# Decay and beta projection as the first, 16-pass unit of a token group, with tile products right behind the value projection

## The reference

```python
proj = rmsnorm(x) @ w_in          # q, k, v, gate z, beta logits (4), decay logits (4), attention q, k, v
qkv  = silu(causal_conv4(q, k, v))
beta = sigmoid(gb)                # 4 heads
g    = -exp(a_log) * softplus(ga + dt_bias)
o_gdn = chunked_delta_rule(q, k, v, g, beta)     # chunks of 64, cumulative sum of g in a chunk
o_gdn = rmsnorm(o_gdn) * silu(z)
o_att = sliding window attention (8 query heads, 2 key heads, window of 2 chunks, sinks)
x = x + concat(o_gdn, o_att) @ w_out
x = x + relu(rmsnorm(x) @ w1)**2 @ w2
```

## Time and profile before

| | us |
|---|---|
| median of 3 runs | 2410.79 (2410.4 to 2412.34) |
| the profiled execution, its own time | 2410.9 |
| its span | 2409.3 |
| TensorE busy in it | 2368.6 (98%) |
| VectorE busy | 1442.3 (60%) |
| ScalarE busy | 959.5 (40%) |

### The profile page before, as it was taken

The page is one execution under the profiler, slowest core; times in us unless marked ns, Lnnn a source line. Parts: engine busy times, 40 slices in busy tenths (PEclk is TensorE's granted clock), DMA queues, the critical chain, the costliest instruction groups (busy, mean ns, idle before and its releaser), DMA issues.

```text
span 2409.3 us, 36625 instructions
## 1 busy us (share of the span) xinstructions
PE 2368.6 (98%) x12654; PEld 1954.2 (81%) x12654; DVE 1442.3 (60%) x2125; ACT 959.5 (40%) x1719; POOL 154.2 (6%) x159
## 2 busy tenths in 40 slices
PE   6999999999999999999999999999999999999998
PEld 4888888888888888888888888888888888888886
DVE  6797662454679765255567966525456885642644
ACT  4476421223357532122346753212234664321222
POOL 0031000000003100000001200000000120000000
PEclk9999999999999999999999999999999999999999
DMA  4211222233321222223332122322432113222241
GB/s 152 96 62 63 96 96 96 96 130 123 106 79 63 80 96 97 96 96 135 118 106 70 63 88 88 104 96 94 141 119 95 68 54 105 88 98 97 92 152 66
DMA packets 63315, 232.63 MB, mean 97 GB/s; under 512 B 7392, under 2 KB 7520, under 8 KB 62544
## 3 DMA queue, kind: packets, MB, share of 16 engines
q1 hardware_dynamic: 55728, 201.98, 25.1%
q0 software_dynamic: 7456, 28.97, 3.5%
HBM read 222.54 MB, written 8.39 MB: 96 GB/s over the span
## 4 chain that ended last, share of the span: by engine, by line
PE 89%; DVE 7%; issue 2%; ACT 2%; DMA 0%; DVEq 0%; POOL 0%; ACTq 0%; POOLq 0%
PE ps L1421 87%; PE ps L1584 1%; PE ps L1647 1%; DVE nq L925 0%; DVE h_l L1357 0%; DVE acc L854 0%; DVE w_l L846 0%; DVE ti L1253 0%; DVE nq_l L930 0%; DVE state L1239 0%; DVE row L972 0%; DVE at L995 0%; DVE at L1011 0%; DVE qkvz L1022 0%; DVE qk L1014 0%
## 5 line engine op out<-in xcount | busy, mean ns | idle before, releaser
L1421 PE MATMUL ps<-h_h,w_h 128*128 128x512 f32 x2004 | 790.7, 395 | 11.3 <-DVE h_l L865 4.4
L1421 PE MATMUL ps<-h_l,w_h 128*128 128x512 f32 x2004 | 781.5, 390 | 0.0
L1421 PE MATMUL ps<-h_h,w_l 128*128 128x512 f32 x2004 | 781.5, 390 | 0.0
L846 DVE TENSOR_TENSOR w_l<-stage,w_h 128x1024 fp32r<-128x1024 f32 x381 | 466.4, 1224 | 256.9 <-ACT w_h L463 243.4
L463 ACT CAST w_h<-stage 128x1024 fp32r<-128x1024 f32 x381 | 398.3, 1045 | 544.2 <-PE ps L1421 543.8
L1421 PEld LDWEIGHTS ps<-h_h,w_h 128*128 128x128 f32 x2004 | 376.9, 188 | 106.7 <-DVE h_l L865 9.0
L1421 PEld LDWEIGHTS ps<-h_h,w_l 128*128 128x128 f32 x2004 | 377.0, 188 | 79.2
L1421 PEld LDWEIGHTS ps<-h_l,w_h 128*128 128x128 f32 x2004 | 377.3, 188 | 77.3 <-issue 1.9
L1421 PE MATMUL ps<-ff_h,w_h 128*128 128x512 f32 x1036 | 404.6, 391 | 0.0
L1421 PE MATMUL ps<-ff_h,w_l 128*128 128x512 f32 x1036 | 403.1, 389 | 0.0
L1421 PE MATMUL ps<-ff_l,w_h 128*128 128x512 f32 x1036 | 403.1, 389 | 0.0
(11 more groups left out here) (196 smaller groups left out, 1884.3 us busy)
## 6 DMA issues: line engine op xcount, KB each, us to landing
stage<-w SPq DMA_DIRECT2D x385, 512.0 KB, 3.3
x_next<-x POOLq DMA_DIRECT2D x20, 512.0 KB, 5.9
out<-xs POOLq DMA_DIRECT2D x32, 256.0 KB, 2.3
xs<-x POOLq DMA_DIRECT2D x8, 512.0 KB, 5.1
xs<-x POOLq DMA_DIRECT2D x4, 1024.0 KB, 5.4
bia<-bias POOLq DMA_DIRECT2D x1, 1024.0 KB, 5.0
cst<-con POOLq DMA_DIRECT2D x1, 448.0 KB, 3.9
cst<-con POOLq DMA_DIRECT2D x1, 192.0 KB, 3.3
```

Source lines behind the costliest of these rows:

```text
L846: dve.tensor_tensor(w_l[:, b, 0:k], stage[:, s, 0:k], w_h[:, b, 0:k].bitcast(F32), ALU.subtract).then_inc(w_lo.sem, 1)
L1421: return pe.matmul(o, a, b, start=start, stop=stop)
```

## The change

BA becomes unit 0 of a group and the convolution units are 1 to 12. BA's weight matrix holds the 8 used columns twice, at 0 to 7 and at 64 to 71; after the split a VectorE copy, `rows_low`, puts the low part of the second copy over columns 64 to 71 of the high buffer. BA then takes two passes per block instead of three (result rows 0 to 7 and 64 to 71, which the row chain adds). The whole row chain with its scans moves to the top of the group on VectorE and ScalarE, ahead of the convolution taps; the low part of convolution unit 1 stands inside it, that of unit 2 in the taps of unit 0. It works on 8 rows instead of 64 or 4. The four transposes of the rows and tile products 0 follow AV, then AK, tile products 1, AQ0, tile products 2, AQ1, tile products 3, AQ2, the 8 value transposes, AQ3. In VectorE's queue the last gate unit's low part moves behind `scatter`, and one pair of norm operations moves into `block_inverse`. ScalarE's load of the silu table moves behind its part of the row chain. The core of the diff (outer indentation taken off):

```diff
...
-U_BA, U_AV, U_AK, U_AQ, U_Z = 12, 13, 14, 15, 19
+U_BA, U_CONV, U_AV, U_AK, U_AQ, U_Z = 0, 1, 13, 14, 15, 19
 U_PAD, U_OUT, U_MLP = 23, 24, 32
...
-        R64, A4 = slice(0, 64), slice(32, 36)
-        X, E, U, L = (rw[R64, i] for i in range(4))
+        R = slice(0, 2 * HEADS)
+        X, E, U, L = (rw[R, i] for i in range(4))
...
+    split_hi(g, 0, 1)
+    act.wait_ge(unit_done.sem, unit_done.after(g, U_BA + 1))
+    act.activation(X, ps[R, A0, :], ACT.Identity, scale=prm[R, C_SGN:C_SGN + 1],
+                   bias=prm[R, C_DT:C_DT + 1]).then_inc(row_act.sem, 1)
+    act.wait_ge(row_dve.sem, row_dve.after(g, 2))
+    act.activation(E, E, ACT.Exp, scale=-1.0).then_inc(row_act.sem, 1)
+    split_hi(g, 0, 2)
+    act.wait_ge(row_dve.sem, row_dve.after(g, 4))
+    act.activation(L, U, ACT.Ln).then_inc(row_act.sem, 1)
+    act.wait_ge(row_act.sem, row_act.after(g, 3))
+    act.activation(U, L, ACT.Exp, scale=-1.0).then_inc(row_act.sem, 1)
...
     act.preload_act_table_set("silu_and_others")
...
+    def conv_input(i, s, split=True):
+        if split:
+            split_hi(g, i * 4, s + 2)
+        act.wait_ge(unit_done.sem, unit_done.after(g, i * 4 + s + 2))
+        act.copy(raw[:, s % 2, 3:], ps[:, A0 + (s + 1) % 2, :]).then_inc(raw_ready.sem, 1)
...
-        conv_input(0, s)
+        conv_input(0, s, s > 0)
...
-    split_hi(g, CONV, U_AV - CONV)
+    split_hi(g, CONV, U_AK - CONV)
...
+    act.wait_ge(vt_ready.sem, vt_ready.after(g, 1))
+    act.copy(avr[:, HD:], ps[:, A0 + 1, :]).then_inc(copied.sem, 1)
     tile(0)
+    split_hi(g, CONV, U_AQ - CONV)
     pack(0)
+    act.wait_ge(unit_done.sem, unit_done.after(g, U_AK + 1))
+    act.copy(akr[:], ps[:, A0, :]).then_inc(copied.sem, 1)
+    norm_hi(0)
+    tile(1)
+    split_hi(g, CONV, U_AQ + 1 - CONV)
...
-        if j < PAIRS - 1:
-            tile(j + 1)
+        if j < 2:
+            tile(j + 2)
         split_hi(g, CONV, U_AQ + 2 + j - CONV)
         norm_root(j)
-        if j < PAIRS - 1:
-            pack(j + 1)
+        if j < 2:
+            pack(j + 2)
+        if j == 2:
+            act.wait_ge(vt_sum.sem, vt_sum.after(g, 1))
+            act.copy(vt[:].rearrange("p c t k -> p c (t k)"), ps[:, PT:PT + 2, :]).then_inc(vt_ready.sem, 1)
     split_hi(g, CONV, U_Z + 2 - CONV)
     norm_root(PAIRS)
...
             pass_pad()
-        if m == GATE - 1:
...
+def rows_low(g, n):
+    own(w_lo, g, n + 1)
+    cols = slice(HD, HD + 2 * HEADS)
+    dve.tensor_copy(w_h[:, 0, :, cols], w_l[:, 0, :, cols].bitcast(F32)).then_inc(ba_lo.sem, 1)
...
 split_lo(0, 0)
+rows_low(0, 0)
 dve.wait_ge(N1["rt_ready"].sem, N1["rt_ready"].after(0, 1))
...
+    rd = [0]
+    def row_step(ins):
+        ins.then_inc(row_dve.sem, 1)
+        rd[0] += 1
+        own(row_dve, g, rd[0])
+    dve.wait_ge(unit_done.sem, unit_done.after(g, U_BA + 1))
+    dve.wait_ge(row_act.sem, row_act.after(g, 1))
+    row_step(dve.scalar_tensor_tensor(out=X, in0=ps[HD:HD + 2 * HEADS, A0, :],
+                                      scalar=prm[R, C_SGN:C_SGN + 1], in1=X, op0=ALU.mult, op1=ALU.add))
+    row_step(dve.scalar_tensor_tensor(out=E, in0=X, scalar=-1.0, in1=X, op0=ALU.mult, op1=ALU.max))
+    dve.wait_ge(row_act.sem, row_act.after(g, 2))
+    row_step(dve.tensor_scalar(U, E, 1.0, None, ALU.add))
+    row_step(dve.scalar_tensor_tensor(out=E, in0=U, scalar=-1.0, in1=E, op0=ALU.add, op1=ALU.subtract))
+    split_lo(g, 0, 2)
+    dve.wait_ge(row_act.sem, row_act.after(g, 4))
+    row_step(dve.tensor_tensor(E, E, U, ALU.mult))
+    row_step(dve.tensor_tensor(L, L, E, ALU.subtract))
+    row_step(dve.scalar_tensor_tensor(out=L, in0=X, scalar=0.0, in1=L, op0=ALU.max, op1=ALU.add))
+    row_step(dve.tensor_scalar(L, L, nalog[R], None, ALU.mult))
+    for t in range(TILES):
+        tile = slice(t * P, t * P + P)
+        row_step(dve.tensor_tensor_scan(row[R, tile], cst[R, K_ONE, :], rw[R, 3, tile], 0.0,
+                                        ALU.mult, ALU.add))
+    row_step(dve.tensor_copy(rowr[64:64 + 2 * HEADS], row[R]))
+    row_step(dve.tensor_tensor(rowr[96:96 + 2 * HEADS], row[R], rowr[64:64 + 2 * HEADS].bitcast(F32),
+                               ALU.subtract))
+    assert rd[0] == row_dve.per_group
+    dve.nop(nofuse=True)
     with dve.Fori(0, CONV // 4) as i:
...
-                    split_lo(g, i * 4, s + 2)
...
+    for t in range(TILES):
+        j = t - 2
         decay(t)
         diagonal(t)
         bias_column(t)
-        norm_square(j + 1)
-        norm_low(j + 1)
+        if t:
+            norm_square(j + 1)
+            norm_low(j + 1)
         products(t)
         split_lo(g, CONV, U_AQ + 2 + j - CONV)
         token_rows(t)
-        norm_apply(j)
+        if j >= 0:
+            norm_apply(j)
...
             if b == 8:
-                split_lo(g, CONV, U_Z + 2 - CONV)
-                norm_apply(PAIRS)
+                query(PAIRS - 1)
+                norm_apply(PAIRS - 1)
...
     gather()
-    query(PAIRS - 1)
-    norm_apply(PAIRS - 1)
+    query(2)
+    norm_apply(2)
     block_inverse()
+    split_lo(g, CONV, U_Z + 2 - CONV)
+    norm_apply(PAIRS)
+    scatter()
     split_lo(g, CONV, U_Z + 3 - CONV)
-    scatter()
...
+        if s == 15:
+            rows_low(g + 1, 0)
...
+    pe.wait_ge(w_lo.sem, w_lo.after(g, 1))
+    pe.wait_ge(ba_lo.sem, ba_lo.after(g, 1))
+    pe.nop(nofuse=True)
+    for k in range(KT):
+        n1_ready(k)
+        mm(ps[:, A0, :], w_h[:, 0, k], h_h[:, k], k == 0, False)
+        last = mm(ps[:, A0, :], w_h[:, 0, k], h_l[:, k], False, k == KT - 1)
+    last.then_inc(unit_done.sem, 1)
...
             pe.wait_ge(raw_ready.sem, raw_ready.after(g, (i * 4 + s) * 3 - 3))
-            unit(g, i * 4, s, A0 + s % 2, hid, first=n1_ready if s == 0 else None)
+            if s == 1:
+                pe.wait_ge(row_dve.sem, row_dve.after(g, 1))
+            unit(g, i * 4, s + 1, A0 + (s + 1) % 2, hid)
...
     pe.wait_ge(raw_ready.sem, raw_ready.after(g, 3 * CONV - 3))
-    unit(g, CONV, U_BA - CONV, A0, hid)
-    pe.wait_ge(raw_ready.sem, raw_ready.after(g, 3 * CONV))
     unit(g, CONV, U_AV - CONV, A0 + 1, hid)
-    pe.wait_ge(row_act.sem, row_act.after(g, 2))
-    unit(g, CONV, U_AK - CONV, A0, hid)
...
+        decay_rows(t)
         if t:
-            decay_rows(t)
...
+    pe.wait_ge(row_dve.sem, row_dve.after(g, row_dve.per_group))
+    pe.nop(nofuse=True)
+    for t in range(TILES):
+        last = pe.transpose(ps[:, ROWT, 64 * t:64 * t + 64], row[0:64, t * P:t * P + P], cst[0:64, K_ID, 0:64])
+    last.then_inc(B1["p_rowt"].sem, 1)
     tile_products(0)
+    pe.wait_ge(raw_ready.sem, raw_ready.after(g, 3 * CONV))
+    unit(g, CONV, U_AK - CONV, A0, hid)
+    tile_products(1)
     for j in range(PAIRS):
-        if j:
-            pe.wait_ge(copied.sem, copied.after(g, j + 1))
-        if j == 1:
-            pe.wait_ge(B1["tok"].sem, B1["tok"].after(g, 1))
+        pe.wait_ge(copied.sem, copied.after(g, j + 1))
         unit(g, CONV, U_AQ + j - CONV, A0 + (U_AQ + j) % 2, hid)
         norm_sum(j)
-        if j < PAIRS - 1:
-            tile_products(j + 1)
+        if j < 2:
+            tile_products(j + 2)
+        if j == 2:
+            wt(B["vb_r"], TILES - 1)
+            wt(B["kd_r"], TILES - 1)
+            for c in range(2):
+                for t in range(TILES):
+                    at = t * P + HD * c
+                    last = pe.transpose(heads(PT + c)[:, t], avr[:, at:at + P], I)
+            last.then_inc(vt_sum.sem, 1)
...
-    wt(B["vb_r"], TILES - 1)
+    pe.wait_ge(vt_ready.sem, vt_ready.after(g, 2))
     last = pe.transpose(ps[:, PT, 0:P], I, I)
...
     for m in range(16):
...
-    ba[:, 32:36] = w_in[:, 2052:2056]
+    ba[:, 4:8] = w_in[:, 2052:2056]
+    ba[:, HD:HD + 2 * HEADS] = ba[:, 0:2 * HEADS]
...
```

More of the change, by code:

```diff
@@ L66 @@
 C_N1, C_N2, C_CONV, C_GN, C_QN, C_KN, C_ALOG, C_DT, C_BLK, C_SINK = 0, 8, 16, 64, 65, 66, 67, 68, 69, 71
-N_PAR = C_SINK + 2 * PAIRS
+C_SGN = C_SINK + 2 * PAIRS
+N_PAR = C_SGN + 1
 K_ID, K_ONE, K_MEAN, K_MEANX, K_HALF, K_CAUS, K_LEV, K_SEL = 0, 1, 2, 3, 4, 5, 6, 7
@@ L185, in build @@
         VROW, KROW = 2, 3
-        VT, ROWT = 0, A0
+        ROWT = NS
         def lev(t):
@@ L489, in _ @@
             act.preload_act_table_set("natural_log_exp_and_others")
-            act.activation(nalog[32:36], prm[32:36, C_ALOG:C_ALOG + 1], ACT.Exp).then_inc(init_act, 1)
+            act.activation(nalog[R], prm[R, C_ALOG:C_ALOG + 1], ACT.Exp).then_inc(init_act, 1)
             act.sem_inc(raw_ready.sem, 6)
@@ L648, in tile @@
                     row_scales(t)
+                act.wait_ge(unit_done.sem, unit_done.after(g, U_AV + 1))
+                act.copy(avr[:, 0:HD], avr[:, TOK:]).then_inc(vt_ready.sem, 1)
+                act.wait_ge(vt_ready.sem, vt_ready.after(g, 1))
+                act.copy(avr[:, HD:], ps[:, A0 + 1, :]).then_inc(copied.sem, 1)
                 tile(0)
+                split_hi(g, CONV, U_AQ - CONV)
                 pack(0)
```

(40 more changed lines are left out.)

90 lines of the change are left out of this document (17 added, 73 removed).

## The result

Eight passes fewer in each group, and the kernel became slower: **2440.2 us** median (2438.33 to 2443.27, 4 runs) against 2410.89 for the kernel before on the same chip (4 runs), ratio 1.0122 (95% interval 1.0104 to 1.0139). The forecast was 2414.9 with a range up to 2418.5. The profiled execution has a span of 2441.7 us, 32.4 more than before's 2409.3, and a mean granted clock of 0.992 where before had 0.998.

The account below looks back on a forecast made before the run. TensorE, busy 98% of the span, was taken to bound the kernel. Waits at group starts +5.4, first group -0.5, behind the convolutions -3.6 and clock +2.7 made +4.0 on 2410.9: 2414.9 us, range 2403 to 2418.5.

Parts of the forecast that it names:

- Passes removed: BA's unit on TensorE: 8 passes fewer in each of four groups, 32 x 0.227 = 7.25 us if all else stays hidden.
- Start of groups 2 to 4: BA 0.4 us late behind `rows_low`; unit 2 waits 3.1 us for its low part; +1.8 us each, +5.4 for three.
- First group: Opening of group 1: passes free of value, unit 0 earlier, unit 2 waiting for its low part; -0.5 us.
- Behind the convolutions: Tile products to gate units: 1.8 us of waits removed, 0.9 of new waits added; -0.9 per group, -3.6 in all.
- Z3's low part, 0.35: Last gate unit: its low part ready 35.0 us after tile 3's start, TensorE there at some 34.3; 0.35 us taken per group.
- GpSimd's queue is unchanged: GpSimd, behind the convolutions: claimed the change leaves its queue as it was; no time was priced for it.
- lateness hidden in the later stages: Rival at `scatter`: Z3's low part 2.91 us later if an add waits for GpSimd's zeroing of `ti`; some 2426; chance 0.03.
- The clock: TensorE behind the new break at unit 2, groups 2 to 4: two falls of three to 1.2 GHz, 1.35 us each, +2.7.
- The sum: Whole kernel: +5.4 - 0.5 - 3.6 + 2.7 = +4.0 us on 2410.9, so 2414.9.
- the faster rival: VectorE's queue at unit 2 quicker than laid out, so the waits and clock falls go: 2401.4 us; chance 0.2.

Follow-up runs that it names:

- the kernel with both orders mended: The changed kernel with Z3's low part back ahead of `scatter` and the row chain's last ten steps spread behind the taps of units 0 to 3: 2400.72 us.

## Why the prediction was wrong, by its steps

**Passes removed: right.** 1.81 us per group in groups 2 to 4, measured alone. In the first group I gave them no value; in the pair of traces that price them they have a negative one, 2.0 us.

**Start of groups 2 to 4: the right wait, 0.8 us a group too small.** `rows_low` made BA 0.49, 0.75 and 0.69 us late (forecast 0.4, from the second group alone). There is no wait at unit 0, whose low part ended at 628.40 for a pass at 628.79, nor at unit 1. Unit 2's wait was forecast at 3.1 us of delay; the idle is 3.24, and the chain's rows stand in the forecast order, the four scans at 1.75 for 1.79. The low part itself ends 19.8 us behind the last pass where 19.2 was forecast, much of it a pause of 0.76 ahead of the taps for which 0.3 was allowed. Unit 2 begins 2.4, 2.7 and 2.6 us later than before (the eight passes taken into account), 7.7 together for the forecast 5.4:

```profile
629.80 0.74 DVE L922 SCALAR_TENSOR_TENSOR rw<-ps,prm,rw 8x512 f32<-8x512 f32 x1 [1.40 <-ACT rw L509]
...
637.09 1.75 DVE L936 TENSOR_TENSOR_SCAN row<-cst,rw 8x128 f32<-8x128 f32 x4
...
639.33 0.69 DVE L939 TENSOR_TENSOR rowr<-row,rowr 8x512 fp32r<-8x512 f32 x1
...
642.10 1.22 DVE L848 TENSOR_TENSOR w_l<-stage,w_h 128x1024 fp32r<-128x1024 f32 x1
```

That it is queueing only, and not work that anyone needs by then, is what the spread chain shows.

**First group: right in sum, by luck.** The scores begin 1.45 us earlier than before; forecast -0.5 for the opening and -1.25 for what lies behind the convolutions (without Z3's 0.35). But the opening brought nothing: AV begins 0.1 us later than before. Unit 0 did begin early, at 30.45, and then ran until 38.9 at the lower pace, so that the forecast wait at unit 2 isn't there. What lies behind gave 1.55.

**Behind the convolutions: the failing step.** The wait for `at` went (1.8 forecast), the value transposes wait 0.34 where 0.35 was forecast. The third term, "Z3's low part, 0.35", is the one that was mis-sized: the step to Z3 grew by 3.6 to 4.5 us, four times together 16.1, and the slow passes behind it made another 8.7. Less the 1.4 forecast, this is 23.4 us of the 28.4 that separate forecast and span. It failed at one place in the text: "from `kd`'s end to the end of `scatter` (762.82 + 2.91) VectorE needed 21.9", to which only the moved work was added. TensorE came to Z3 34.1 us after tile 3's start (forecast 34.3), but the low part was there after 37.6 or 38.5 us (forecast 35.0), by the two patterns. I carried the durations over from rows in which no GpSimd operation ran beside `scatter`'s pairs, and moved a GpSimd job of 3.8 us on top of them without pricing that; pairs and low part together are 4.0 or 3.1 us longer. "GpSimd's queue is unchanged" was true of its order and false of its times: it is released by the `norm_apply` that I saw move. The rival "lateness hidden in the later stages" named the right place and the right job, the zeroing, with a chance of 0.03 and the wrong mechanism: it looked for a wait of the `ti` addition, and the operations beside the MEMSET were the ones that paid.

That it is this contention, the rows show by dose: the first pair takes 0.79 beside no MEMSET, 1.63 with 1.1 us of one over it, 2.35 beside one, 4.10 beside two, and the same pair in the kernel before grows when only the release of the MEMSETs moves. The low part's 1.91 beside GpSimd's COPY is the second form of it. The Trainium skill states this (SBUF — State Buffer, section SBUF: two separate sides): VectorE and GpSimd share a port pair under an exclusive lock, a VectorE operation in one of its faster two-port modes, or with two SBUF inputs beside a GpSimd operation that reads SBUF, and the GpSimd operation shut each other out. The rows agree with it: the TENSOR_SCALAR with one tensor input is stopped by a MEMSET, which reads nothing, for about as long as that lasts; a TENSOR_TENSOR of `block_inverse` beside the same MEMSETs took 1.10 and 1.16, where the kernel with the moved `norm_apply` has 1.04 and 1.12 without them; a TENSOR_TENSOR beside the COPY was stretched. The MEMSETs themselves took 1.81 to 2.00 in all cases, so nearly all the waiting here is VectorE's. That the low part's stretch is the COPY's doing rests on these rows alone; no run took the COPY away from it without moving the low part.

**The clock: the mechanism right, the size too small, and a place missed.** Two falls of 1.35 were forecast; it fell behind unit 2 in all three groups (1.8, 2.7 and 1.8 us lost) and behind all four breaks at Z3. The 1.35 from the earlier trace rows was the low end: a fall costs 1.6 to 2.9 us where dense passes follow, and some 3 to 9.4 where short products with waits follow, as at `masked`. The Trainium skill's rule that I weighed (TensorE: Matmul & The Clock Gate, section HAM oscillation) points the right way, fewer breaks, fewer falls. Read strictly, as I did for the other sum, it would have kept the clock behind the 3.24 us at unit 2, as behind the 1.2 to 1.3 us at `masked`; the rows of after and of the kernel with the moved `norm_apply` don't agree with that reading. The breaks at Z3 in after, 3.6 to 4.4 us, are longer than the one it was read for and don't decide it.

**The sum.** Forecast +4.0. Add 23.4 for Z3 (16.1 + 8.7 - 1.4), 3.5 for the clock behind unit 2 (6.2 for 2.7), 2.3 for unit 2's later start (7.7 for 5.4) and 0.6 for the first group's opening (+0.1 for -0.5). Take off 1.1, since behind the convolutions 6.1 us were gained where 5.0 were forecast: +32.7, as in the table, against +32.4 of the span. One bound of the prediction doesn't follow from its own terms: two falls of the clock and no gain behind the convolutions make 2418.5, not 2415.7; the measured time is far outside either. The time given to the faster rival, 2401.4, is nearly what the kernel with both orders mended reached, 2400.7, though by another way: there the waits went because the chain was spread, not because the queue was quicker.

**A version that beats both kernels** is `z3_tail_rows`: Z3's low part ahead of `scatter`, the row chain's tail spread over the taps, `rows_low` ahead of the addition, 2399.4 us, 0.48% under the kernel before. By the rows above, a third pass per block in the first group alone would bring up to 2 us more in some executions; that wasn't tried.

## What to carry to other kernels

When a step is moved in VectorE's queue, look at GpSimd too, not only at that queue: what does this step release on GpSimd, and which VectorE operations will now stand beside that? And put the operand that the busiest engine needs next (here a weight's low part) ahead of every chain that has time, even where it saves only one unit: a chain can be spread, a break on TensorE costs its own length and can cost a fall of the clock. A forecast for a move has to sum the queue with durations measured beside the same neighbours, or give the range the price of their contention.

## What the runs showed of the hardware

- A fall of the clock behind a break is not certain at 2.2 to 3.2 us of idle: behind breaks of the same kind it fell three of three times in one execution (after, unit 2), one of three in another (Z3's low part first, same unit), and with one MEMSET moved two of three times there and two of four with 2.17 us idle at Z3. Behind 1.07 and 1.72 us amid dense passes it didn't fall; behind 1.2 to 1.3 us at `masked`, where short products follow, it fell in three of four groups of one execution, with some 3 to 9.4 us lost, where a fall amid dense passes cost 1.6 to 2.9. So in these traces a fall's price went with what TensorE did behind it.
- In the first group, where input paces TensorE, the number of passes per block goes with the clock: with three per 1.39 us it rose within the unit (at 24.6 us in three of three traces), with two it rose behind the unit (29.3 to 36.6 us in seven traces), and where extra products had raised it beforehand it fell again (at 23.7).
- VectorE and GpSimd: with both patterns in one execution (pairs of 4.10 and 0.57 in groups 2 and 4, of 2.33 and 1.48 in groups 1 and 3) the same contention cost 3.3 or 2.5 us, by whether VectorE came in between the two MEMSETs.
